# Moving the mLSTM gates into the page loop of the latent attention, and putting the w_uv products on column groups

## The reference

```python
# latent attention of the sample tokens over 8 cached pages of 128 rows for each of 8 sequences
p = softmax(q . k * scale);  o_lat = p @ latent;  h_b = einsum('bqhc,chv->bqhv', o_lat, w_uv)

# gates of the mLSTM (8 heads)
log_i = 15*tanh(i_pre/15);   log_f = log_sigmoid(15*tanh(f_pre/15))
bcum = cumsum(log_f);  m_row = maximum(bcum + m, max over s <= l of (bcum_l - bcum_s + log_i_s))
w = exp(bcum_l - bcum_s + log_i_s - m_row);  w_state = exp(bcum + m - m_row)
m_new = maximum(b_last + m, max(b_last - bcum + log_i));  wk, decay = exp(... - m_new)
# then, for each head: z = xn @ w_in[...], the masked products q.k, w.v and the new C and n
```

## Time and profile before

| | us |
|---|---|
| median of 3 runs | 3180.69 (3180.51 to 3186.72) |
| the profiled execution, its own time | 3179.73 |
| its span, first to last instruction | 3177.9 |
| mean granted TensorE clock | 0.965 |

### The profile page before, as it was taken

The page is one execution under the profiler, slowest core; times in us unless marked ns, Lnnn a source line. Parts: engine busy times, 40 slices in busy tenths (PEclk is TensorE's granted clock), DMA queues, the critical chain, the costliest instruction groups (busy, mean ns, idle before and its releaser), DMA issues. The chain is left out here.

```text
span 3177.9 us, 49812 instructions
## 1 busy us (share of the span) xinstructions
PE 3005.0 (95%) x19234; PEld 2698.1 (85%) x19234; DVE 1394.4 (44%) x2031; ACT 1164.5 (37%) x1890; POOL 253.4 (8%) x369
## 2 busy tenths in 40 slices
PE   8997999999999996999997999999799999999996
PEld 7655788888888884899987999989699999999995
DVE  4263333333333323455453344443566644666543
ACT  5225332232223221345443443332455533445331
POOL 0000000000000000000000000000133300333202
PEclk9999999999999995999998999999899999999997
DMA  7422301101100103555645555555355546555452
GB/s 226 144 83 81 113 1 31 31 1 31 30 24 7 31 1 113 163 170 179 190 149 155 168 158 146 167 153 173 105 159 166 153 140 177 171 162 169 127 163 68
DMA packets 617360, 371.35 MB, mean 117 GB/s; under 512 B 24362, under 2 KB 599148, under 8 KB 615448
## 3 DMA queue, kind: packets, MB, share of 16 engines
q1 hardware_dynamic: 606344, 359.20, 38.0%
q10 hardware_dynamic: 9472, 9.44, 0.8%
q0 software_dynamic: 1408, 0.82, 0.1%
HBM read 346.67 MB, written 22.75 MB: 116 GB/s over the span
## 5 line engine op out<-in xcount | busy, mean ns | idle before, releaser
L266 DVE TENSOR_TENSOR w_lo_b<-stage,w_hi_b 128x2048 fp32r<-128x2048 f32 (+1 forms) x280 | 599.1, 2140 | 592.2 <-ACT w_hi_b L259 592.2
L276 PE MATMUL bank<-xnH,w_hi_b 128*128 128x288 f32 x2688 | 730.6, 301 | 21.3 <-PEq L2354 18.5
L277 PE MATMUL bank<-xnL,w_hi_b 128*128 128x288 f32 x2688 | 725.9, 296 | 0.0
L259 ACT ACTIVATE w_hi_b<-stage 128x2048 fp32r<-128x2048 f32 (+1 forms) x280 | 500.7, 1788 | 538.3 <-PE bank L281 515.3
L276 PEld LDWEIGHTS bank<-xnH,w_hi_b 128*128 128x128 f32 x2688 | 508.9, 189 | 31.9 <-issue 31.7
L277 PEld LDWEIGHTS bank<-xnL,w_hi_b 128*128 128x128 f32 x2688 | 507.9, 189 | 0.2
L1357 PE MATMUL bank<-ukH,latH 128*128 128x512 f32 x1024 | 404.9, 395 | 0.0
L1359 PE MATMUL bank<-ukH,latL 128*128 128x512 f32 x1024 | 399.4, 390 | 0.0
L1358 PE MATMUL bank<-ukL,latH 128*128 128x512 f32 x1024 | 398.5, 389 | 0.0
L276 PE MATMUL bank<-haH,w_hi_b 128*128 128x288 f32 x1280 | 355.1, 304 | 34.4 <-DVE axL L2547 13.2
L281 PE MATMUL bank<-xnH,w_lo_b 128*128 128x288 f32 x2688 | 384.8, 296 | 0.0
(11 more groups left out here) (446 smaller groups left out, 3069.7 us busy)
## 6 DMA issues: line engine op xcount, KB each, us to landing
stage<-in_w_in_dram SPq DMA_DIRECT2D x88, 1024.0 KB, 5.2
stage<-in_w_up_dram SPq DMA_DIRECT2D x88, 1024.0 KB, 5.4
stage<-in_w_down_dram SPq DMA_DIRECT2D x64, 704.0 KB, 4.4
latf<-in_cache_kv_latent_dram SPq DMA_DIRECT2D x64, 256.0 KB, 2.6
stage<-in_w_branch_a_dram SPq DMA_DIRECT2D x16, 1024.0 KB, 5.4
stage<-in_w_branch_b_dram SPq DMA_DIRECT2D x16, 1024.0 KB, 5.4
stage<-in_w_out_dram SPq DMA_DIRECT2D x16, 1024.0 KB, 5.5
stage<-in_w_uk_dram SPq DMA_DIRECT2D x8, 1024.0 KB, 5.0
```

The costliest lines, as they stand in the source:

```text
L259: act.activation(h, a, ACT.Copy).then_inc(w_hi, 1)
L266: dve.tensor_tensor(lo, a, h.bitcast(F32), ALU.subtract).then_inc(w_lo, 1)
L276: pe.matmul(out, hi, xH(k), start=first and k == 0, stop=False)
L277: pe.matmul(out, hi, xL(k), start=False, stop=False)
```

## The change

Five things are changed.

1. The gate block is gone. Its work runs inside the page block's first batch, where there is no softmax of an earlier batch to do, and in its free PSUM bank 6. Pieces of it (`gates(j)` in each engine's code) stand after page j: ACT at pages 0 and 5, PE at 1, 2, 4 and 7, DVE at 1, 2, 3, 4, 6 and 7. The five memsets and the addition of the bias stand ahead of DVE's first `lo`, with a wait for the six small loads, which SP issues after four pages.
2. The running maxima are computed with the heads on 8 partitions and time along the row: 8 steps in which each element is compared with the one 1, 2, 4, ... 128 places before, and two such steps for the samples.
3. The w_uv products have `olat` as the stationary operand (32 columns) and 128 columns of w_uv moving, with four heads side by side on four groups of 32 columns of the array. The result comes out with rows and columns exchanged, so it is copied to SBUF, turned by four transposes, and copied again. w_uv is loaded in four column blocks: two into stage slots early, two into the page buffer late.
4. For the last batch the products with the values come before the denominators, and two dummy activations load the tables of ACT ahead of use.
5. xn and the high and low weight parts have one place for the whole kernel; tiles of the front and the page block lie in the same place. xn is reloaded and weight blocks 0 to 3 of the head stage are loaded within the page block, and block 0 is split there. The constant table loses `pick`, `seen_s`, `same_neg` and two thirds of `seen`.

```diff
 SP, page block
                     for j in range(HALF):
                         load(At(0), j)
+                    sp.dma_start(gb[:], ...).then_inc(g_in, 16)
+                    for s in range(S_S):
+                        sp.dma_start(m0s[s:N_S:S_S, :], ...).then_inc(g_in, 16)
+                    sp.dma_start(n_rows, ...).then_inc(g_in, 16)
                     for j in range(HALF, NPG):
                         load(At(0), j)
                     sp.wait_ge(uk_lo, 4)
-                    for k in range(LC):
-                        sp.dma_start(stage[:, k, :], A["w_uv"][0, k * P:(k + 1) * P]...).then_inc(uv_in, 16)
+                    for j in range(2):
+                        uv_load(j)
+                    for m in range(2):
+                        head_load(sp, At(0), m)
...
-                    sp.wait_ge(f_hev, BH)
+                    sp.wait_ge(g_cp, 2)
+                    store(sp, O["mlstm_m_p"][0], m_out[0:1, 0, :])
+                    store(sp, O["mlstm_m_s"][0], m_out[0:N_S:S_S, 1, :])
+                    sp.wait_ge(f_o, NJ * (NB - 1))
+                    for j in range(2, 4):
+                        uv_load(j)
+                    sp.wait_ge(n_k, 4 * NPG * NB)
+                    sp.dma_start(xnH[:].bitcast(F32), xnH_dram).then_inc(xn_back, 16)
+                    sp.dma_start(xnL[:].bitcast(F32), xnL_dram).then_inc(xn_back, 16)
+                    sp.wait_ge(f_uv, 4)
+                    for m in range(2, 4):
+                        head_load(sp, At(0), m)
+                    sp.wait_ge(f_hev, 2)
                     sp.dma_start(hb_dram[:, :, S_P:], hs[:]).then_inc(e_st[0], 16)
 PE, gates(j): after the scores of page 1 the matmuls that stood at lines 1715 to 1723 and one transpose,
 after page 2 three transposes (L1726 before), after page 4 six, after page 7 the matmuls of lines 1739 to 1742
+                        if j == 1:
+                            pe.wait_ge(g_act, 4)
...
+                        if j == 2:
+                            pe.wait_ge(g_a, 1)
...
 PE, after the loop
-                    denominators(At(NB - 1))
-                    values(At(NB - 1), 0, NJ)
+                    values(At(NB - 1), 0, NJ, last=True)      # waits for f_ex, not for f_rs
+                    last_denominators(At(NB - 1))             # bank 5 instead of 6
                     turn_out(At(NB - 1))
...
-                    for h in range(BH):
-                        need(pe, f_hev, h - 1)
+                    for j in range(4):
                         for k in range(LC):
-                            mm = pe.matmul(bank[h % 2][:, 0:N_S], stage[:, k, h * BV:(h + 1) * BV], olat[:, k, h, :], start=k == 0, stop=k == LC - 1)
-                        mm.then_inc(f_h, 1)
+                            for g in range(4):
+                                mm = pe.matmul(bank[j // 2][g * N_S:(g + 1) * N_S, j % 2 * P:(j % 2 + 1) * P], olat[:, k, 4 * j + g, :],
+                                               uv_of(j)[:, k, g * BV:(g + 1) * BV], start=k == 0, stop=k == LC - 1)
+                        mm.then_inc(f_uv, 1)
+                    for i, ready in enumerate((f_hq, f_hq2)):
+                        pe.wait_ge(ready, 1)
+                        for j in range(2):
+                            tr = pe.transpose(bank[2 + i][:, j * P:(j + 1) * P], ol[:, (2 * i + j) * P:(2 * i + j + 1) * P], ident)
+                        tr.then_inc(f_h, 1)
 DVE
+                    for t_ in (ga[:], nb_[:], dif[:], M[:], run):
+                        dve.memset(t_, 0.0).then_inc(g_z, 1)
+                    dve.wait_ge(g_z, 5)
+                    dve.wait_ge(g_in, 16 * 6)
+                    dve.tensor_tensor(g3[:], gate_tok[:], gb[:]..., ALU.add).then_inc(g_cp, 1)
                     lo(At(0), 0)
...
 DVE, gates(j)
+                        if j == 2:
+                            dve.wait_ge(g_pe, 2)
...
+                                for s in range(4 * i, 4 * i + 4):
+                                    src, dst = run[:, s % 2], run[:, 1 - s % 2]
+                                    vo.step(dve, dve.tensor_tensor(dst[:, P:], src[:, P:], src[:, P - (1 << s):P + S_P - (1 << s)], ALU.max))
...
+                    dve.wait_ge(f_uv, 2)
+                    dve.tensor_copy(ol[:, 0:2 * P], bank[0][:, 0:2 * P]).then_inc(f_hq, 1)
+                    split_lo(dve, At(N0))
 ACT
+                    act.wait_ge(f_uv, 4)
+                    act.activation(ol[:, 2 * P:], bank[1][:, 0:2 * P], ACT.Copy).then_inc(f_hq2, 1)
+                    for i in range(2):
+                        act.wait_ge(f_h, i + 1)
+                        act.activation(hs[:, 8 * i:8 * i + 8, :]..., bank[2 + i][:, 0:2 * P], ACT.Copy).then_inc(f_hev, 1)
+                    split_hi(act, At(N0))
```

More of the change, by code:

```diff
@@ L11 @@
 from contextlib import ExitStack
+import math
 import numpy as np
@@ L1398, in denominators, with last_denominators @@
                         pe.matmul(bank[6][HQ:, 0:1], psums[:, b.mod(2), :], ones[:, 0:1], start=True, stop=True).then_inc(f_sum, 1)
-                    def values(b, j0, j1):
+                    def last_denominators(b):
+                        pe.wait_ge(f_ps, b.of(1, 1))
+                        pe.matmul(bank[5][0:HQ, 0:1], psums[:, b.mod(2), :], ones[:, 0:1], start=True, stop=True)
+                        pe.matmul(bank[5][HQ:, 0:1], psums[:, b.mod(2), :], ones[:, 0:1], start=True, stop=True).then_inc(f_sum, 1)
@@ L1401, in values @@
+                    def values(b, j0, j1, last=False):
                         a = b.mod(2)
-                        if j0 == 0:
+                        if last:
+                            pe.wait_ge(f_ex, b.of(2, 2))
+                        elif j0 == 0:
                             pe.wait_ge(f_rs, b.of(1, 1))
@@ L1435, in batch @@
                                 turn_out(b - 1)
+                            if not post:
+                                gates(j)
                     pe.transpose(bank[6][0:ROPE, 0:N_S], krr[0:N_S, 2, :], ident[0:N_S, 0:N_S]).then_inc(f_kt, 1)
@@ L1491, in batch, with gates @@
                                 exps(b - 1)
+                            if last and j == 2:
+                                act.activation(dum[:], eps, ACT.Sqrt)
+                            if not post:
+                                gates(j)
                         root(b)
+                        if last:
+                            act.activation(dum[:], eps, ACT.Exp)
+                    def gates(j):
+                        if j == 0:
+                            act.wait_ge(g_cp, 1)
+                            act.activation(g3[:], g3[:], ACT.Tanh, scale=1.0 / CAP).then_inc(g_act, 1)
+                            act.wait_ge(g_act, 1)
+                            act.activation(nlf[:], g3[:, :, AH:], ACT.Exp, scale=-CAP).then_inc(g_act, 1)
+                            act.wait_ge(g_act, 2)
+                            act.activation(nlf[:], nlf[:], ACT.Ln, bias=ones[:, 0:1]).then_inc(g_act, 1)
+                            act.activation(li[:], g3[:, :, 0:AH], ACT.Copy, scale=CAP).then_inc(g_act, 1)
+                        if j == 5:
+                            act.wait_ge(g_cp, 2)
+                            act.activation(dif[:], dif[:], ACT.Exp).then_inc(g_act, 1)
                     act.wait_ge(f_kt, 1)
```

330 lines of the change are left out of this document (148 added, 182 removed).

## The result

| | us |
|---|---|
| before, median of 4 runs | 3183.01 (3180.51 to 3186.72) |
| after, median of 4 runs | 3147.07 (3145.41 to 3150.52) |
| ratio | 0.9888, 95% interval 0.987 to 0.9905 |
| profiled execution of after | 3150.52, span 3148.7, clock 0.972 |

The kernel is 36 us faster. I had forecast 3133.5 with a range of 3124 to 3145: the time lies 2 us above the range. About a quarter of the gain that I forecast is missing.

The account below looks back on a forecast made before the run. PE, busy 3005.0 of 3177.9 us, was taken as the bound, with a dependent chain after the page loop. Terms summed to -47.2 from 3179.73, giving 3132.6; with 1.0 for the median, 3133.5 us, range 3124 to 3145.

Parts of the forecast that it names:

- Other edits: nothing: Reload of xn, stores of m, early w_uv loads and smaller constant table: no cost or gain counted.
- Gate block, first split: Between store and head block: gate block removed, -33.9 us; block 0 split while the store is under way, -1.9.
- Last batch and w_uv: After the page loop: values ahead of denominators, net -1.35 us; w_uv products, copies and transposes, -18.7.
- The store behind two loads: Store of hs queued behind weight loads 2 and 3: lands 8.0 us after its issue, +4.5 us.
- Its rival: Store of hs not held back: lands 3.5 us after its issue, total 3129 us; chance 15%.
- Gates in the first batch: Gate products on PE in the page loop: 6.9 us at half clock, 3.4 at full, so +3.4 us.
- PE loses its clock in the first batch: PE waits in gates at pages 2, 4, 7; half clock for six pages costs 81 us, total 3214; chance 2%.
- Gates on DVE and ACT: Gate work on DVE and ACT in the page loop: hidden by the keys, costs nothing.
- Start of the block: Start of page block: DVE waits for six small loads before the low part of page 0, keys later by +0.8 us.
- the rival that they do not overlap: w_uv products: four column groups run one after another, stage keeps 26.5 us, 20 us lost, total 3153; chance 6%.

## Why the prediction was wrong

The step that failed is **"Other edits: nothing"**. I had listed there transfers and the smaller constant table, and asked of each only when it happens. That the same edits give every tile another start, and that a matmul's pace could hang on it, I did not weigh, neither as a term nor as a rival. The runs showed in its place that moved tiles slow the key matmuls, by 17.2 us in all (22.2 in the loop less 4.95 for the gates); 1024 groups at 19 ns make 19.5, from the medians. With it taken away by 224 bytes and nothing else, the kernel stands at 3135.63 us, 2 above the forecast, and 47.9 below the runs of before beside it, where my sum was -47.2. That this comes so close is partly luck, as gates and clock cost more than I had and the tail less. The 2 us by which the time lies above the range say little by themselves: I had taken 3180.69 for the kernel before, and with a fourth run its median is 3183.01. Against that the gain is 35.9 us, 11.3 short of my sum; the loop is what shows the step to be wrong.

Point by point:

- *Gate block, first split:* right. Store to head block -29.6 (forecast -29.4), first product 1.9 earlier (-1.9).
- *Last batch and w_uv:* right. Both together -21.4 against -20.05. The products took 5.4 us, between full and half clock as assumed (6.5), and the copies and transposes 1.3 (1.6). The clock in this chain differs from execution to execution: last keys to store took 24.33 to 28.08 us in the kernels with groups.
- *The store behind two loads:* right, 7.8 us where I had 8.0; turned round, it lands after 3.7. Its rival falls.
- *Gates in the first batch:* 4.95 instead of 3.4; 3.6 where the clock held, so the term was right and the fall came on top. The rival "PE loses its clock in the first batch" was half right. I argued that it could come only where PE waits. PE did not wait, and the clock fell all the same in four of six kernels, at or just behind small products in a row; but it came back after some 4 us, and cost 1.4 to 1.6, not 81.
- *Gates on DVE and ACT:* hidden, as forecast; PE waits for none of `ga`, `MT` and `dif`.
- *Start of the block:* forecast +0.8, measured nothing: from the block's first matmul to the first keys 16.2 us before (315.07 to 331.28), 15.95 after (318.69 to 334.64). The first `ukL` starts 13.4 and 13.5 us behind that matmul, so the small loads cost next to nothing.
- *Column groups:* the rival that they do not overlap falls: the products took 5.4 us, where it had 26.5.

What stays open: why the start modulo 256 matters, and whether any distance besides 0 is quick (32, 64, 128 and 224 are not, and no others were tried); how the three spacings of 233, 239 and 228 ns come about where only `latL` is off; why the clock falls in some executions at the end of the attention, or at the sums of the gates, and not in others; what the exchange of the operands gives without the groups.

## What to carry to other kernels

When a change moves tiles, compare the start-to-start spacing of the matmuls that it does not touch, before looking at those it does: a loop of thousands of like instructions turns 6 ns into 20 us. Where 512-column matmuls with a new stationary operand each set the pace, let the stationary and the moving operand start at the same place modulo 256 bytes; one unused tile does it. For products of 288 columns that was no help here. Before a difference of a few us in one stage is put down to a change, look at the granted clock of that stage in several kernels with the same code. On a queue, put the small transfer that somebody waits for ahead of the large ones that nobody waits for yet.

## What the runs showed of the hardware

- At full clock, three matmuls of 128x512, each with its own weights, take 681 ns where the stationary and the moving tiles start alike modulo 256 bytes, and 693 to 702 where they do not (distances of 32, 64, 128 and 224, for one or for all three matmuls): 2 to 3% of that work. Products of 288 columns moved by 1 to 4 ns at most, and not by that rule.
- The granted clock can fall to half with PE busy for all of the time. It did so at or within 1 us behind nine products with 8 to 64 moving columns in a row, in four kernels of six, and was back at full some 4 us later; in two kernels with the same products it stayed at full, and so it did in two in which seven of them were spread among 512-column matmuls.
- A store of 256 KB in small pieces landed 3.4 to 3.7 us after its issue with two loads of 1 MB behind it on the queue (four kernels), and 7.6 to 7.9 us with the two ahead of it (four kernels).
